# Up projections: part of the low-part subtractions of two weight units moved from VectorE to GpSimd

## The reference

```
D_FF = 5632
def swiglu(hn, w_in, w_out):            # hn (256, 2048), w_in (2048, 2*5632), w_out (5632, 2048)
    u = hn @ w_in
    return (jax.nn.silu(u[..., :D_FF]) * u[..., D_FF:]) @ w_out
...
h = h + swiglu(rmsnorm(h, norm_ffn[layer]), ffn_w_in[layer], ffn_w_out[layer])
```

## Time and profile before

| What | Value |
|---|---|
| Median of three runs | 1991.75 us (1991.08 to 1991.82) |
| Span of the profiled execution | 1990.0 us |
| TensorE busy | 1970.1 us (99%) |
| VectorE busy | 1654.2 us (83%) |
| ScalarE busy | 1140.1 us (57%) |
| GpSimd busy | 78.3 us (4%) |
| Granted TensorE clock | 1.000 |
| Share of matmul line L1753 in the chain that ended last | 74.2% |
| L1017 in `raw_lo`, 128x2048 | 176 times, 2288 ns each |

### The profile page before, as it was taken

How to read it: one execution, slowest core, us unless ns; L and a number is a source line. 1 busy time by engine, 2 the same in 40 slices (tenths; PEclk the granted TensorE clock), 3 DMA queues, 4 the chain that set the end, 5 groups by cost and what they waited for, 6 DMA issues and landing times.

```text
span 1990.0 us, 25234 instructions
## 1 busy us (share of the span) xinstructions
PE 1970.1 (99%) x9395; PEld 1656.1 (83%) x9395; DVE 1654.2 (83%) x1881; ACT 1140.1 (57%) x1372; POOL 78.3 (4%) x113
## 2 busy tenths in 40 slices
PE   7999999999999999999999999999999999999999
PEld 6898888888888888888898888888888888888887
DVE  6968655788988889999977886469888888999897
ACT  5478545555555556556676664555555655656564
POOL 1040200000000000000002110000000000000000
PEclk9999999999999999999999999999999999999999
DMA  7564663665665655656565335356566566655554
GB/s 279 170 212 150 239 202 106 195 207 191 195 205 191 208 191 192 209 191 211 196 210 163 120 127 190 121 177 204 196 197 204 191 196 203 200 195 199 202 199 168
DMA packets 159485, 378.17 MB, mean 190 GB/s; under 512 B 6154, under 2 KB 10516, under 8 KB 159028
## 3 DMA queue, kind: packets, MB, share of 16 engines
q1 hardware_dynamic: 158960, 376.02, 56.7%
q0 software_dynamic: 272, 1.13, 0.2%
q10 hardware_dynamic: 180, 0.05, 0.0%
HBM read 375.08 MB, written 2.10 MB: 190 GB/s over the span
## 4 chain that ended last, share of the span: by engine, by line
PE 88%; issue 5%; DVE 3%; ACT 2%; DMA 1%; POOL 1%; POOLq 0%; SPq 0%; DVEq 0%; ACTq 0%
PE bank L1753 74%; PE bank L1950 6%; PE bank L1948 3%; PE bank L1714 2%; PE bank L1746 1%; PE bank L1934 1%; DMA raw<-in_ffn_w_in 1%; PE bank L1737 1%; DVE w_lo L1017 0%; PE bank L1947 0%; POOL stats L1698 0%; DMA h<-in_x 0%; ACT w_hi L562 0%; ACT gtmp L694 0%; DMA raw<-in_ffn_w_out 0%
## 5 line engine op out<-in xcount | busy, mean ns | idle before, releaser
L1753 PE MATMUL bank<-w_hi,act 128*128 128x512 f32 x3680 | 1173.9, 390 | 1.7 <-issue 1.5
L1753 PEld LDWEIGHTS bank<-w_hi,act 128*128 128x128 f32 x3680 | 690.8, 188 | 147.0 <-issue 2.3
L562 ACT ACTIVATE w_hi<-raw 128x2048 fp32r<-128x2048 f32 (+2 forms) x271 | 509.6, 1883 | 326.7 <-DMA raw<-in_ffn_w_in 151.0
L1753 PE MATMUL bank<-raw_lo,act 128*128 128x512 f32 x1584 | 616.3, 389 | 0.0
L1017 DVE TENSOR_TENSOR raw_lo<-raw,w_hi 128x2048 fp32r<-128x2048 f32 x176 | 402.2, 2288 | 110.8 <-ACT w_hi L562 108.6
L1753 PEld LDWEIGHTS bank<-raw_lo,act 128*128 128x128 f32 x1584 | 297.5, 188 | 60.5
L1017 DVE TENSOR_TENSOR w_lo<-raw,w_hi 128x2048 fp32r<-128x2048 f32 (+2 forms) x95 | 206.8, 2188 | 82.8 <-ACT w_hi L562 82.7
L1067 DVE TENSOR_TENSOR raw_lo<-raw,w_hi 128x2048 fp32r<-128x2048 f32 x88 | 201.0, 2284 | 0.0
L1753 PE MATMUL bank<-w_lo,act 128*128 128x512 f32 x520 | 173.8, 389 | 0.0
L1950 PE MATMUL bank<-act,w_hi 128*128 128x512 f32 x480 | 169.1, 397 | 0.0
L625 ACT ACTIVATE w_hi<-raw 128x1024 fp32r<-128x1024 f32 x88 | 93.0, 1057 | 131.9 <-DMA raw<-in_ffn_w_in 121.1
(11 more groups left out here) (227 smaller groups left out, 2004.3 us busy)
## 6 DMA issues: line engine op xcount, KB each, us to landing
raw<-in_ffn_w_in SPq DMA_DIRECT2D x176, 1024.0 KB, 5.4
raw<-in_ffn_w_out SPq DMA_DIRECT2D x88, 1024.0 KB, 4.9
raw<-in_lru_w_in SPq DMA_DIRECT2D x32, 1024.0 KB, 5.3
raw<-in_lru_w_out SPq DMA_DIRECT2D x16, 1024.0 KB, 5.4
raw<-in_w_o SPq DMA_DIRECT2D x16, 1024.0 KB, 4.9
raw<-in_w_ukv SPq DMA_DIRECT2D x8, 1024.0 KB, 5.3
raw<-in_w_uq SPq DMA_DIRECT2D x8, 768.0 KB, 4.7
raw<-in_w_dkv SPq DMA_DIRECT2D x8, 576.0 KB, 4.6
```

The source lines that it names most:

```text
L562: A.activation(flat_chunk(w_hi, s, size), flat_chunk(raw, s, size), ACT.Copy).then_inc(w_hi_done, 1)
L1753: i = T.matmul(bank[:, :], x_part, w_part, start=first and n == 0, stop=last and n == 2)
```

## The change

GpSimd takes the two odd row tiles (128x1024) of the low part of units 0 and 1, in blocks 2 to 10 of both up projections: 2 x 9 x 2 = 36 instructions. VectorE's instruction for those units shrinks to the two even tiles. GpSimd begins with unit 0 after ScalarE's bank copy of the block before (`p1_done`), and with unit 1 after the last unit of the block before (`chunk_used`). TensorE waits for GpSimd in the middle of units 0 and 1, between even and odd tiles. Its first two bodies are written out in front of the loop, which now has four turns. The GpSimd loop of the first up projection stands between two `rstd` calls.

```diff
+POOL_UNITS = 2 * (FB - 2)
...
+        def odd_tiles(buf, s):
+            return buf[s][:, 1:KC:2, :]
+        def pool_lo_needed(f, i, u):
+            return 2 * i + (POOL_UNITS * f + u - 3)
...
 (VectorE, following)
+                    elif u < 2 and not (isinstance(i, int) and i == 1):
+                        dve.wait_ge(w_hi_done, 4 * m + s + 1)
+                        V.tensor_tensor(raw_lo[s][:, 0:KC:2, :], raw[s][:, 0:KC:2, :],
+                                        w_hi[s][:, 0:KC:2, :].bitcast(F32), ALU.subtract).then_inc(w_lo_done, 1)
...
 (GpSimd)
-            for d in (0, 1):
-                pool.wait_ge(ms_done, d + 1)
-                rstd(SS_T, RS + 2 * (d + 1), 2, D, rstd_done)
+            def low_halves(f, c0):
+                with pool.Fori(1, FB - 1) as i:
+                    for u in range(2):
+                        pool.wait_ge(w_hi_done, 8 * i + (c0 + 8 + u + 1))
+                        if u == 0:
+                            pool.wait_ge(p1_done, i + SUM_BLOCKS * f)
+                        else:
+                            pool.wait_ge(chunk_used, 8 * i + (c0 + 8))
+                        G.tensor_tensor(odd_tiles(raw_lo, u), odd_tiles(raw, u), odd_tiles(w_hi, u).bitcast(F32),
+                                        ALU.subtract).then_inc(pool_lo, 1)
+            pool.wait_ge(ms_done, 1)
+            rstd(SS_T, RS + 2, 2, D, rstd_done)
+            low_halves(0, C_UP0)
+            pool.wait_ge(ms_done, 2)
+            rstd(SS_T, RS + 4, 2, D, rstd_done)
...
             rstd(SS_T, RS + 6, 2, D, rstd_done)
+            low_halves(1, C_UP1)
...
 (TensorE, body of up)
-                        elif u == 1:
-                            plain_unit(u, 2 * u, result, False, False, (0,))
-                            transpose_g(i + FB * f, shared[0:2])
+                        elif u < 2:
+                            plain_unit(u, 2 * u, result, u == 0, False, (0,))
+                            if u == 1:
+                                transpose_g(i + FB * f, shared[0:2])
+                            if not (isinstance(i, int) and i == 1):
+                                pe.wait_ge(pool_lo, pool_lo_needed(f, i, u))
                             e = plain_unit(u, 2 * u, result, False, False, (1,))
...
-                with pe.Fori(0, S_BLOCKS // 2) as j:
+                body(1, True)
+                body(2, False)
+                with pe.Fori(1, S_BLOCKS // 2) as j:
```

More of the change, by code:

```diff
@@ L282, in build_program @@
         h_shared = sem("h_shared")
+        pool_lo = sem("pool_lo")
         out_ready = sem("out_ready")
```

## The result

The changed kernel takes 2017.03 us (median of four runs, 2016.90 to 2017.65), the kernel before on the same chip 1991.41 us: a ratio of 1.0131, 95% interval 1.0118 to 1.0143. That is 25.6 us slower. The profiled execution has a span of 2015.9 us against 1990.0, 25.9 more.

What follows compares the result with a forecast made beforehand. TensorE, without a gap, was taken to bound the up projection blocks; 2.02 us delay less 0.60 lead gives 1.4 us, times 18 is 25.2; span 1990.0 becomes 2015, median 2017 us. Range 1991 to 2023.

Steps and rivals of the forecast that it cites:

- No gain is possible: Up projection blocks where the change acts: TensorE has no gap, so an earlier low part saves 0 us.
- VectorE's half: Units 0 and 1: halved subtractions save VectorE 1.07 us each, 36 times; about 0.1 us of lead, no time gained.
- GpSimd's price: GpSimd's 128x1024 subtraction takes 2.36 us; TensorE's new waits for it and the written-out bodies cost nothing.
- Who is first: At unit 2's sums: GpSimd starts at about 697.35, VectorE at 697.48, so GpSimd comes first, narrowly at one end.
- the rival's condition: Condition of the no-change rival (0.18): GpSimd's hold begins over 0.13 us after its start, so VectorE is first at 697.48.
- The delay and the lead: Sums of unit 2 start 2.02 us late; less 0.60 us lead, TensorE stands 1.4 us in each of 18 blocks.
- `shared_add` is not held: Beside unit 0's GpSimd instruction: VectorE's `shared_add`, reading PSUM and one SBUF tensor, is taken as not delayed, still 0.69 us.
- No change: Rival at unit 2's sums: VectorE keeps its way, GpSimd works beside the result bank reads; 1991.8 us, chance 0.18.
- Some blocks only: Rival: GpSimd wins the narrow race in half of the blocks, 13 us lost; about 2004 us, chance 0.14.
- more: Rival: `shared_add` is held up too, 2.0 us a block, 36 us in all; 2028 us, chance 0.10.
- faster: Rival: unseen TensorE losses or a shorter end of block 10 give less than 1 us; 1990 us, chance 0.05.

Runs made afterwards that it cites:

- unit 0 alone: Changed kernel, but GpSimd takes the odd tiles of unit 0 only and unit 1 is VectorE's again: 1991.30 us, ratio 1.0000 to the kernel before.
- after the sums: Changed kernel, but GpSimd starts unit 1 only when VectorE has finished the four sums of unit 2: 1991.35 us, ratio 1.0001 to the kernel before.
- the kernel with one tile: Changed kernel, but for unit 1 GpSimd takes one row tile (128x512) and VectorE three: 1995.69 us, ratio 1.0021 to the kernel before.
- Three tiles: Changed kernel, but for unit 1 GpSimd takes three row tiles (128x1536) and VectorE one: 2042.95 us, ratio 1.0259 to the kernel before.
- the kernel with unit 1 alone: Changed kernel, but GpSimd takes the odd tiles of unit 1 only and unit 0 is VectorE's again: 2017.13 us, ratio 1.013 to the kernel before.
- Four memsets of GpSimd in a row: Kernel before, plus idle GpSimd memsets after a one-element subtraction in the second up projection, from unit 7's end: 1991.43 us, ratio 1.0000.

## Why the prediction was right, point by point

- *No gain is possible.* Right. The kernels with GpSimd out of the way (unit 0 alone, after the sums) stand at 1.0000 and 1.0001, at the period of 42.38 us.
- *VectorE's half.* A small term was mis-sized. I put the earlier start of the sums at about 0.1 us; the kernel with one tile shows 0.25. It did not matter in the 15 blocks of the changed kernel where GpSimd is first, because GpSimd's end sets the sums there.
- *GpSimd's price.* Estimate 2.36 us, measured 2.41 (median of 36). Three tiles took 3.52 and one 1.3 to 1.4 when GpSimd was first.
- *Who is first.* Forecast GpSimd, narrowly; it was, in 15 of 18 blocks. The margin can be very small: in the kernel with unit 1 alone GpSimd's record begins at 751.32 and VectorE's at 751.33, and VectorE is held all the same (2.94 us). So the rival's condition, a hold that begins over 0.13 us after GpSimd's start, is not met. For the three others the prediction said that GpSimd would slip in at the 0.04 us gap before the third sum. It slips in before the second, without any gap, and the period is nearly the same (43.72 to 43.79 us).
- *The delay and the lead.* Delay 2.02 forecast; lead 0.60. The stall came out at 43.84 - 42.38 = 1.46 us in place of 1.4, with 0.82 us of it as idle time before the transposes in place of 0.9; with the lead of 0.60 that is a delay of 2.06. Over all blocks the mean stall is 1.45 us in the first up projection and, where a block took 42.41 us before, 1.43 in the second: 9 x 1.45 + 9 x 1.43 = 25.9 us, which is what the spans differ by. That the median agrees with the 2017 to 0.1 us is partly luck, as the sum had 25.2 us and the kernel before was put at 1991.75.
- *`shared_add` is not held.* Right: 0.69 us beside GpSimd in every kernel.
- *Rivals.* "No change" falls, also where VectorE is first: what it needed was that GpSimd be kept out of a queue of back-to-back instructions, and GpSimd is not. "Some blocks only", "more" and "faster" did not occur.

The one row that spoke for the rival, GpSimd's 9.12 us at 116.17, stays unexplained. There GpSimd did not get in for 8 us between VectorE instructions with two SBUF inputs; here it got in at once each time. It wasn't tried apart.

## What to carry to other kernels

Before work goes to GpSimd, look at what VectorE executes in those microseconds in its queue, not at what the semaphore's name suggests: in these runs instructions that read PSUM and one SBUF tensor ran beside it at their usual 0.69 us, and those with two SBUF inputs stood until 0.15 us before it ended, up to 2.25 us beside an instruction of 2.41. Then ask for the lead of whatever is queued behind: here 0.6 us, so 2 us of standing cost 1.46 in each of 18 blocks. And relieving an engine earns nothing while the bounding engine has no gap that waits for it: the same share moved without harm gave 1.0001.

## What the runs showed of the hardware that I had not expected

- GpSimd gets in between two VectorE instructions that follow on each other without a gap (750.50 and 751.11 above; 13 of 18 blocks of the kernel with one tile).
- A wait of 1.9 us of TensorE in every block let the granted clock fall after 5 of 18 such waits in the kernel with three tiles, at 1.2 us each time. In the block shown the clock is still 1.00 while TensorE waits and in the first 0.9 us behind the wait (500.1 to 501.0), and falls after that. Waits of 0.8 us in the changed kernel never did. Of the 51.9 us between the spans of that kernel and of the one before, 18 x 2.55 = 45.9 are the stalls and 5 x 1.2 = 6.0 the clock.
- Four memsets of GpSimd in a row (1457.21 to 1458.54), right on VectorE's two-input sums, did not slow these (0.69 and 0.68 us).
